# The second attention of a three-attention kernel: values as the stationary operand, weights divided before their turn, and one PSUM copy moved

## The reference, cut to what matters

```python
    def block(blk, qb):
        sc = jnp.einsum('bqhd,bkhd->bhqk', qb, k).astype(jnp.float32) * scale
        p = causal_softmax(sc, blk, s)
        return jnp.einsum('bhqk,bkhd->bqhd', p.astype(v.dtype), v)

    o = query_block_map(block, q)
    return o.reshape(b, s, MLA_HEADS * MLA_V) @ w_out
```

## Time and profile before

| | |
|---|---|
| median of 3 runs | 1506.28 us (1506.09 to 1506.65) |
| the profiled execution: its own time | 1505.69 us |
| the profiled execution: span of the profile | 1504.0 us |
| PE busy | 1304.8 us (87%), 9738 matmul records |
| DVE busy | 664.4 us (44%) |
| ACT busy | 274.0 us (18%) |
| POOL busy | 131.4 us (9%) |
| HBM read | 511.39 MB, 341 GB/s over the span |
| second attention, first score to start of L465 | 661.5 to 697.5 us |

### The profile page before, as it was taken

One profiled execution on the slowest core, in us unless ns is written; L12 is line 12 of the kernel. 1 busy time (PEld: TensorE's weight loads), 2 busy tenths in 40 slices (PEclk: granted clock), 3 DMA queues, 4 the chain that ended last, 5 costly groups with the idle time before them and its releaser, 6 DMA issues.

```text
span 1504.0 us, 25662 instructions
## 1 busy us (share of the span) xinstructions
PE 1304.8 (87%) x9738; PEld 807.2 (54%) x9738; DVE 664.4 (44%) x1621; ACT 274.0 (18%) x756; POOL 131.4 (9%) x201
## 2 busy tenths in 40 slices
PE   9999999766776679999999766776678999999997
PEld 4455565433443444665665433443344874899943
DVE  3874534221222123672634221222122635699976
ACT  2153211100010001372211100010001134222200
POOL 1312000000000000210100000000000143222100
PEclk9999999898898899999999998898889999999999
DMA  8978799999999999959899999999999991654400
GB/s 287 404 286 340 290 421 404 421 421 422 422 422 422 422 422 396 364 195 420 320 420 404 421 421 422 422 422 422 422 422 400 381 364 44 210 169 169 168 29 28
DMA packets 120555, 513.63 MB, mean 342 GB/s; under 512 B 12296, under 2 KB 46796, under 8 KB 69144
## 3 DMA queue, kind: packets, MB, share of 16 engines
q1 hardware_dynamic: 118576, 507.30, 84.4%
q0 software_dynamic: 1728, 5.12, 0.9%
q10 hardware_dynamic: 168, 0.09, 0.0%
HBM read 511.39 MB, written 1.08 MB: 341 GB/s over the span
## 4 chain that ended last, share of the span: by engine, by line
PE 53%; DMA 20%; SPq 18%; DVE 3%; issue 3%; POOL 1%; ACT 1%; ACTq 0%; POOLq 0%; DVEq 0%
DMA ring<-in_moe_w_up 14%; SPq L1872 13%; PE bank L1415 9%; PE bank L2678 8%; PE bank L575 7%; PE bank L2713 4%; DMA BC<-in_moe_w_up 3%; PE bank L1430 3%; PE bank L1401 3%; PE bank L453 3%; PE bank L2303 3%; PE bank L465 3%; SPq L1881 3%; PE bank L1443 2%; DMA ring<-in_moe_w_down 2%
## 5 line engine op out<-in xcount | busy, mean ns | idle before, releaser
L1415 PE MATMUL bank<-ring,hT 128*32 128x256 f32 (+1 forms) x2848 | 280.5, 461 | 133.4 <-DMA ring<-in_moe_w_up 70.3
L1415 PEld LDWEIGHTS bank<-ring,hT 128*32 128x32 f32 (+1 forms) x2848 | 148.5, 133 | 238.9 <-issue 180.7
L1707 DVE TENSOR_SCALAR pT<-pT 128x256 f32<-128x256 f32 x34 | 10.0, 294 | 407.4 <-ACT pT L1839 407.4
L1415 PE MATMUL bank<-BC,hT 128*32 128x256 f32 (+1 forms) x1120 | 138.6, 410 | 41.8 <-DMA ring<-in_moe_w_up 24.3
L1401 PEld LDWEIGHTS bank<-gtab,hn 128*128 128x128 f32 x1088 | 129.3, 192 | 15.4 <-issue 14.3
L1401 PE MATMUL bank<-gtab,hn 128*128 128x128 f32 x1088 | 132.6, 275 | 0.1
L1430 PE MATMUL bank<-ring,gtab 128*32 128x512 f32 (+1 forms) x768 | 116.8, 596 | 1.9 <-DMA ring<-in_moe_w_down 1.4
L1443 PE MATMUL bank<-hT,A 128*128 128x512 f32 x256 | 118.3, 605 | 0.0
L1415 PEld LDWEIGHTS bank<-BC,hT 128*32 128x32 f32 (+1 forms) x1120 | 72.1, 120 | 76.2 <-issue 57.4
L575 PE MATMUL bank<-ring,hT 128*128 128x512 f32 (+3 forms) x288 | 99.9, 505 | 0.7 <-DMA ring<-in_diff_w_in 0.4
L1839 ACT ACTIVATE pT<-bank 128x256 f32<-128x256 f32 x34 | 13.1, 384 | 460.5 <-PE bank L1415 460.5
(11 more groups left out here) (390 smaller groups left out, 1942.3 us busy)
## 6 DMA issues: line engine op xcount, KB each, us to landing
ring<-in_moe_w_gate SPq DMA_DIRECT2D x90, 1024.0 KB, 25.1
ring<-in_moe_w_up SPq DMA_DIRECT2D x88, 1024.0 KB, 25.5
ring<-in_moe_w_down SPq DMA_DIRECT2D x88, 1024.0 KB, 26.2
BC<-in_moe_w_gate SPq DMA_DIRECT2D x38, 1024.0 KB, 24.8
BC<-in_moe_w_up SPq DMA_DIRECT2D x32, 1024.0 KB, 25.0
BC<-in_moe_w_down SPq DMA_DIRECT2D x28, 1024.0 KB, 26.6
ring<-in_w_ada SPq DMA_DIRECT2D x24, 1024.0 KB, 13.9
ring<-in_w_up SPq DMA_DIRECT2D x22, 1024.0 KB, 7.6
```

The source lines that it names most:

```text
L1415: i = nc.tensor.matmul(GATE[q * cap:(q + 1) * cap, part * FF:(part + 1) * FF], xg[:, c, q * cap:(q + 1) * cap], u[:, c, :], start=(c == 0) ...
```

## The change

Two edits. The output stage of the second attention gets `by_channel=True`, which switches `turn`, `sum_v`, `weigh`, `store`, the order of DVE's loop, and the output stage over to the other form described above. And in a stage by channel the copy of K7 moves from behind `mask(1)` to behind `mask(2)`.

```diff
@@ -844,7 +844,7 @@
                 if last_turned:
                     last_turned(dve, 0)
                 mask(1)
-                if last_turned:
+                if last_turned and not by_channel:
                     last_turned(dve, 1)
                 weigh(0)
                 for i in range(items):
@@ -856,6 +856,8 @@
                         mask(i + 2)
                     if not by_channel and i + 1 < items:
                         weigh(i + 1)
+                    if last_turned and by_channel and i == 0:
+                        last_turned(dve, 1)
                     if beside:
                         beside.vector(dve, i)
                     out.vector(dve, i)
@@ -2173,7 +2175,7 @@
                      for x in (nopeT, peT)]
             return [pairs], lambda kt, m: v_l[:, kt, h, :]
         cond2.plan(5)
-        o2 = OutStage(square_units(t["mla_w_out"][0], D, order="(c p)"), add_x)
+        o2 = OutStage(square_units(t["mla_w_out"][0], D, order="(c p)"), add_x, by_channel=True)
         a2 = attention_stage("a2", latents_ready, [latent_head(h) for h in range(HEADS)], MLA_QK ** -0.5, causal_bias, o2,
                              head_turned=latent_head_turned, last_turned=last_keys_turned)
```

## The result

The changed kernel takes **1508.89 us** (median of 18 runs, 1508.33 to 1509.95); the kernel before took 1506.20 in the same comparison (18 runs). The ratio is 1.0019, 95% interval [1.0012, 1.0026]: 2.7 us slower. The prediction said 1505.8 with a range up to 1508.2, so it was wrong, in sign too. The profiled execution took 1508.66 us, with a span of 1506.9.

What follows compares the result with a forecast made beforehand. It took PE's attention loop, through the gate `ordered`, then the full DMA stream as the bound. Removed transposes -1.75 and start plus loop +1.27 gave about -0.5 us: 1505.8 us, range 1504.0 to 1508.2.

Steps and rivals of the forecast that it cites:

- The transposes removed, 1.75: Second attention: 16 transposes of the heads (L420) leave PE's full chain, a gain of 1.75 us.
- the start of 0.80: Start of the second attention: the first transpose now waits for the division and goes out 0.80 us later, at about 663.82.
- The loop of 1.28 us between DVE and ACT: Attention before item 5: rounds of 1.28 us replace 1.06; start and loop together cost 1.27, item 5's transpose at 670.03.
- The price of a division, 0.20: DVE in the second attention: each division taken as 0.20 us of spacing; upper bound 0.29 more for each of five.
- The last items covered: Last three items of the attention, without scores: weights reckoned ready in time; up to 0.5 us if that cover went.
- The gates: SP's first gate opens 5.4 us later, at 679.0; 17 loads end at 724.6, leaving 1.8 us of slack before `ordered`.
- Rival B: Second mixture's loads: the stream released late ends after `ordered`; 1509.4 us at twice the delay; chance of over 0.2% slower 0.06.
- Rival D: Slower division, last three items uncovered, or a stream that eats its slack: +0.5 to +3, 1506.8 to 1509.3; chance 0.17.
- Second edit: Attention's start: K7's two instructions left in front would add their time to the first transpose; L662 alone lasts 0.47 us.
- the bytes left at 734, so the end moves one to one with the gate: DMA from 734 to 1150 us, busy without a break: the end follows the gate `ordered`, SP's first load at 731.57.

Runs made afterwards that it cites:

- before_gate13: Kernel before, with the first gate of the second mixture's loads on SP's queue tied to item 13's scores instead of item 11's: 1505.86 us against 1505.83, ratio 1.0000.
- the padding pair: Kernel before with 26 or 56 float32 matmuls added in the first mixture's overflow branch, which never runs: 1512.19 and 1514.72 us.
- after_shim4: Changed kernel with 1 small matmul (4 instructions) executed just ahead of the second mixture's expert loop: 1509.62 us, ratio 1.0024.
- after_shim32: Changed kernel with 8 small matmuls (32 instructions) executed just ahead of the second mixture's expert loop: 1507.28 us, ratio 1.0009.
- after_gap32: Changed kernel with 8 small matmuls (32 instructions) executed in the second mixture's first block, where PE waits for DVE: 1505.09 us against 1506.26, ratio 0.9994.
- after_pad8: Changed kernel with 8 float32 matmuls (32 instructions) added in the first mixture's overflow branch, which never runs: 1508.95 us, ratio 1.0017.

## Why the prediction was wrong

Point by point, by its own steps:

- *The transposes removed, 1.75, and the start of 0.80:* right. The first transpose went out at 663.86; 663.82 was predicted. The 1.75 is borne out by the net below.
- *The loop of 1.28 us between DVE and ACT:* right, 1.26 measured (transposes at 667.29, 668.54, 669.80); item 5 at 669.80 against 670.03, so start and loop cost 1.04 where 1.27 stood. Net -0.7 (1.04 - 1.75) where -0.5 was the sum, and -0.7 is what the marks above give.
- *The price of a division, 0.20:* right. In the round shown above the mask starts 0.20 behind the division, whose record lasts 0.29. By the Trainium skill, "VectorE: DVE Perf Modes", section "Terms", the next instruction waits for an empty pipe; by the records the two overlap here as well.
- *The last items covered:* right. PE waited for no division after item 0.
- *The gates:* right in time (679.01 against 679.0), and the stream kept its slack, though less than the 1.8 us reckoned, and with a wrong end: 724.6 was expected, but the DMA share was still 0.90 at 728 to 730 us. In the kernel before DMA had not ended at 719.2 either; it took up the loads issued at 720.34 and 720.77 and was busy again until 727. POOL's tables were ready at 708.13, not 708.9. `before_gate13` shows that this delay costs nothing. Rival B had the right sign and the wrong mechanism.
- *Rival D:* its range, 1506.8 to 1509.3, holds the measured 1508.89 by luck. None of its three mechanisms occurred: no slower division, no uncovered item, no stream without slack. The prediction also took 0.2%, 3.0 us, for what can be told from no change; the interval of the result is 0.07% to either side, and 2.7 us stand clear of it.
- *Second edit:* it spares 0.5 us at `ordered` (the first transpose comes 0.7 earlier behind the mark: 8.17 against 8.88 us), as K7's two instructions stand behind the division. The prediction had named only L662's 0.47 for it.
- **The step that failed** is the sentence that from 734 to 1150 us the time is "the bytes left at 734, so the end moves one to one with the gate". It took those bytes as given, and PE behind 734 as without effect on the stream. The change altered both: 17 packets of instructions more, two returns of the loop that lasted 6.1 us instead of 0.21, and, just behind each, a wait of PE of 4.5 us. The prediction counted the 32 instructions removed from PE as time and never as length of a program that a hardware loop follows.

How the 3.7 us are made up is only partly shown. Between 820 and 1120 us the weights' queue moved 0.60 MB less; at 422 GB/s that is 1.4 us, of which the instructions' 0.28 MB take 0.7. PE's waits delay the slots it frees: SP's loads of three `up` blocks behind the first return went out from 912.16 where they had gone out from 907.87, 4.3 later; at 992.84 against 991.72 it was 1.1. No run separated the share of the bytes from that of the waits, so the rest stays open. What is shown is the cause: the padding pair (+2.5 us), `after_shim4` against `after_shim32` (2.3) and `after_gap32` against the changed kernel (3.8, in two comparisons, each beside the kernel before: 1.0019 and 0.9994) all turn on 7 or 8 packets, and so does the branch's record in every one of the twenty profiles, with the edits or without.

## What to carry to other kernels

Behind an edit that changes how many instructions an engine issues, look at where the later hardware loops of that engine begin and end, at the packets of the instruction queue in them and at the records of their branches, before the edit is judged: here the edits were worth 0.7 us and the shift of the code cost 3.8. A control that adds instructions needs a place of its own too; here padding in a skipped branch moved the jump's landing, and matmuls put where DMA's share dipped beside full neighbours, so that PE set the pace, were not free and, at 26, came with a lower clock. With the code's place held, a gain of half a microsecond in a stage can be read from two marks of the trace more surely than from medians: the marks repeated within 0.05 us, the medians' intervals are some 3 us wide.

## What the runs showed of the hardware

- A loop of 1656 instructions on PE that touches 7 packets of 16 KB ran its iterations with no instruction packet from 900 to 1140 us; one that touches 8 fetched 17 there, its two branches back lasted 6.15 and 6.08 us instead of 0.21, and it waited 4.58 and 4.45 us just behind them. The Trainium skill, "Runtime: NRT & Kernel Launch", section "Instruction fetch mechanics", gives PE a buffer of 128 KiB (2048 instructions) refilled in 16 KiB blocks, and in the same section says that the buffer is only two lines and that a taken branch to a target outside them forces a fetch. The first statement fits, if one of its eight blocks is kept for the next; no run shows that directly. The two lines do not: a buffer of two lines would have refetched the loop of 7 in every iteration, and its branch, whose target lies six packets back, took 0.21 us. That a taken branch can wait for a fetch agrees, by the 6.1 us.
- At the jump over the padded branch PE waited 4.4 us when it landed in the next packet (its record lasted 6.2 us instead of 0.35), and up to 3.1 us shortly behind it when it landed near the end of its own; at 18.79 it waited for nothing. `after_pad8` spread over 5.5 us, the changed kernel over 1.6; that the wait varied between executions is argued from this, since each kernel has one profile.
- The place at which the loop goes from 8 packets to 7 was between instructions 7407 and 7423 of the count used here, not at 7424. The places of the waits narrow it down: 7411, and the five instructions with which the loop's body opens ahead of its first matmul, make 7416.
- In the control with 26 matmuls of 16 columns in a row the granted clock fell from 1.00 to 0.50 (804 to 812 us); with 8 of them it stayed at 1.00.
